# First mixer's recurrence: half a value product put between levels 0 and 1, two modulation chunks summed behind level 8, queries ahead of weight splits

## The reference, cut to what matters

```python
ada = jnp.einsum('bd,lde->lbe', jax.nn.silu(c), w_ada) + b_ada[:, None, :]   # 6 x 1024 modulation values
...
q = split_heads(jax.nn.silu(p[..., 3 * w:4 * w]), HG_HEADS) * (HG_DIM ** -0.5)
o_f, h_f = chunk_gla(q, k_f, v, logf_f, h0_f)          # S_t = diag(f_t) S_{t-1} + k_t v_t^T, o_t = S_t^T q_t
o_b, h_b = chunk_gla(flip_t(q), flip_t(k_b), flip_t(v), flip_t(logf_b), h0_b)
o = rmsnorm(o_f + flip_t(o_b), hg_gain.reshape(HG_HEADS, 1, HG_DIM))
o_hg = merge_heads(o) * jax.nn.silu(p[..., 4 * w:5 * w])
o_mlp = chunk_sgu(p[..., 5 * w:5 * w + MLP_WIDTH], p[..., 5 * w + MLP_WIDTH:], sgu_g, sgu_b, w_s, b_s)
...
x = x + g1 * (concatenate([o_hg, o_mlp]) @ w_out)
```

## Time and profile before

| what | value |
| --- | --- |
| median of 3 runs | 962.12 us (959.48 to 964.09) |
| the profiled execution | 960.85 us, span 959.0 us |
| TensorE busy | 927.3 us (97%) |
| VectorE busy | 740.5 us (77%) |
| ScalarE busy | 476.0 us (50%) |
| mean granted clock of TensorE | 0.995 |
| recurrence, level 0 to level 8 | 99.00 to 158.76 us of the span |

### The profile page before, as it was taken

The page is one execution under the profiler, slowest core; times in us unless marked ns, Lnnn a source line. Parts: engine busy times, 40 slices in busy tenths (PEclk is TensorE's granted clock), DMA queues, the critical chain, the costliest instruction groups (busy, mean ns, idle before and its releaser), DMA issues.

```text
span 959.0 us, 18956 instructions
## 1 busy us (share of the span) xinstructions
PE 927.3 (97%) x8174; PEld 872.4 (91%) x8174; DVE 740.5 (77%) x1101; ACT 476.0 (50%) x571; POOL 14.8 (2%) x34
## 2 busy tenths in 40 slices
PE   5999899999989999999999999999999999999997
PEld 3689899999989999989999899999999999999986
DVE  3689998889898988867957985535676987887863
ACT  3454445636545565458663753334645443334363
POOL 0000000002000000000200000000000000000000
PEclk8999999999999999999999999999999999999999
DMA  9988354465548656424654334333254565556541
GB/s 338 352 285 271 127 176 133 133 209 173 176 155 272 233 171 226 176 89 176 218 190 162 107 128 137 130 132 131 91 194 163 192 196 195 181 177 203 183 141 45
DMA packets 114051, 171.84 MB, mean 179 GB/s; under 512 B 3240, under 2 KB 96704, under 8 KB 109872
## 3 DMA queue, kind: packets, MB, share of 16 engines
q1 hardware_dynamic: 111680, 165.63, 51.4%
q0 software_dynamic: 1088, 2.57, 0.9%
q10 hardware_dynamic: 1200, 2.43, 0.7%
HBM read 169.55 MB, written 1.06 MB: 178 GB/s over the span
## 4 chain that ended last, share of the span: by engine, by line
PE 64%; DVE 8%; ACT 4%; issue 3%; DVEq 0%; ACTq 0%
PE bank L1171 20%; PE bank L1172 19%; PE bank L1173 19%; DVE wlo L629 3%; PE bank L1746 2%; ACT whi L620 2%; DVE arena L2307 1%; ACT arena L981 1%; DVE arena L2393 1%; DVE arena L1973 0%; DVE XT L2259 0%; PE bank L1280 0%; DVE raw L2049 0%; ACT arena L851 0%; PE bank L1210 0%
## 5 line engine op out<-in xcount | busy, mean ns | idle before, releaser
L1171 PE MATMUL bank<-hhi,whi 128*128 128x256 f32 (+1 forms) x1744 | 507.1, 291 | 7.5 <-issue 1.8
L1172 PE MATMUL bank<-hlo,whi 128*128 128x256 f32 (+1 forms) x1744 | 500.2, 287 | 0.0
L1173 PE MATMUL bank<-hhi,wlo 128*128 128x256 f32 (+1 forms) x1744 | 500.1, 287 | 0.0
L629 DVE TENSOR_TENSOR wlo<-raw,whi 128x2048 fp32r<-128x2048 f32 x131 | 299.7, 2289 | 109.7 <-ACT whi L620 84.1
L1171 PEld LDWEIGHTS bank<-hhi,whi 128*128 128x128 f32 x1744 | 334.0, 192 | 17.0 <-issue 11.9
L1172 PEld LDWEIGHTS bank<-hlo,whi 128*128 128x128 f32 x1744 | 334.2, 192 | 4.1 <-issue 1.2
L1173 PEld LDWEIGHTS bank<-hhi,wlo 128*128 128x128 f32 x1744 | 334.1, 192 | 2.5
L620 ACT ACTIVATE whi<-raw 128x2048 fp32r<-128x2048 f32 x131 | 250.1, 1913 | 139.7 <-PE bank L1173 127.3
L1171 PE MATMUL bank<-whi,hhi 128*128 128x256 f32 (+1 forms) x256 | 87.8, 343 | 0.8 <-ACT arena L1131 0.8
L1172 PE MATMUL bank<-wlo,hhi 128*128 128x256 f32 (+1 forms) x256 | 86.7, 339 | 0.0
L1173 PE MATMUL bank<-whi,hlo 128*128 128x256 f32 (+1 forms) x256 | 86.5, 338 | 0.0
(11 more groups left out here) (364 smaller groups left out, 805.9 us busy)
## 6 DMA issues: line engine op xcount, KB each, us to landing
raw<-in_w_up_dram SPq DMA_DIRECT2D x44, 1024.0 KB, 5.1
raw<-in_w_in_tiles_dram SPq DMA_DIRECT2D x32, 1024.0 KB, 4.9
raw<-in_w_down_dram SPq DMA_DIRECT2D x22, 1024.0 KB, 4.9
raw<-in_w_ada_dram SPq DMA_DIRECT2D x19, 1024.0 KB, 5.3
raw<-in_w_in_dram SPq DMA_DIRECT2D x14, 1024.0 KB, 5.3
raw<-in_w_branch_dram SPq DMA_DIRECT2D x6, 1024.0 KB, 5.1
arena<-in_w_ada_dram SPq DMA_DIRECT2D x10, 512.0 KB, 9.5
raw<-in_w_out_dram SPq DMA_DIRECT2D x4, 1024.0 KB, 5.1
```

What stands on the lines that cost most here:

```text
L629: dve.tensor_tensor(wlo[:, g % RING, :], raw[:, n % RING, :], whi[:, g % RING, :].bitcast(F32), ALU.subtract).then_inc(w_lo, 1)
L1171: pe.matmul(o, wh, ah, start=start, stop=False, **kw)
L1172: pe.matmul(o, wh, al, start=False, stop=False, **kw)
L1173: return pe.matmul(o, wl, ah, start=False, stop=stop, **kw)
```

## The change

Nothing is added or left out: the same instructions run in another order, on four engines.

1. TensorE: the first 24 of the 48 matmuls of v0a go between level 0 (with `ada_unit(2)`) and level 1, the other 24 stay behind level 1.
2. ScalarE: the split for q1's successor (mv0) and the copy of wsT go behind `mix_keys(1)`.
3. VectorE: the splits of mv0, mv1 and mu1 go from ahead of levels 2, 3 and 6 to behind these levels, that of gt0 from ahead of level 7 to behind level 8, that of gt1 from ahead of the normalisation of MV to behind it; level 7 goes ahead of `statistics(1)`; `weighted_late(15)` and `weighted_late(16)`, which stood behind levels 2 and 3, go behind level 8, the first right behind it, the second behind the normalisation of MV.
4. SyncE: the chunks 15 and 16 go three places back in the list each, which then reads mv1, mu0, mu1, 15, gt0, 16, gt1, 17.

```diff
@@ the list of chunks @@
-    for name in ("ff0", "ff1", "fb0", 8, "fb1", 9, 10, "q0", 11, "q1", 12, 13, 14, "v0", "v1", "mv0", 15, "mv1", 16,
-                 "mu0", "mu1", "gt0", "gt1", 17, "wo0", "wo1", "wo2", 18, "wo3", 19):
+    for name in ("ff0", "ff1", "fb0", 8, "fb1", 9, 10, "q0", 11, "q1", 12, 13, 14, "v0", "v1", "mv0", "mv1", "mu0",
+                 "mu1", 15, "gt0", 16, "gt1", 17, "wo0", "wo1", "wo2", 18, "wo3", 19):
@@ ScalarE @@
             for c in range(2):
                 unit_act(f"q{c}", Q[:, 2 * c:2 * c + 2, :], ACT.Silu)
-                split_hi(act, G[f"q{c}"] + RING)
                 if c == 0:
+                    split_hi(act, G["q0"] + RING)
                     tok_keys(0)
-            m_wait("wsT")
-            act.activation(wsT, m_bank("wsT")[:, :].rearrange("p (h q) -> p h q", h=HEADS), ACT.Copy
-                           ).then_inc(m_empty["act"], 1)
...
             mix_keys(1)
+            split_hi(act, G["q1"] + RING)
+            m_wait("wsT")
+            act.activation(wsT, m_bank("wsT")[:, :].rearrange("p (h q) -> p h q", h=HEADS), ACT.Copy
+                           ).then_inc(m_empty["act"], 1)
@@ TensorE @@
-            def gemm_tok(name, w, unit=None, t0=0):
+            def gemm_tok(name, w, unit=None, t0=0, part=(0, 1)):
 
                 wh, wl = w_parts(name, KT)
-                bk = g_open(unit or name)
-                for n in range(2):
+                bk = g_open(unit or name) if part[0] == 0 else g_bank(unit or name)
+                for n in part:
...
-                ins.then_inc(g_full, 1)
+                if part[-1] == 1:
+                    ins.then_inc(g_full, 1)
...
             level(0)
             ada_unit(2)
+            gemm_tok("v0", 512, "v0a", 0, part=(0,))
             level(1)
-            gemm_tok("v0", 512, "v0a", 0)
+            gemm_tok("v0", 512, "v0a", 0, part=(1,))
             level(2)
@@ VectorE @@
             level(1)
             modulation(2, g_wait("A2"), g_empty["dve"])
-            split_lo(dve, G["q1"] + RING)
             values(0, 0)
             level(2)
-            weighted_late(15)
+            split_lo(dve, G["q1"] + RING)
             values(0, 1)
+            level(3)
             split_lo(dve, G["v0"] + RING)
-            level(3)
-            weighted_late(16)
             values(1, 0)
...
             statistics(0)
+            level(6)
             split_lo(dve, G["mv0"] + RING)
-            level(6)
+            level(7)
             link(statistics(1))
...
             ins.then_inc(sg_stats, 1)
+            level(8)
+            weighted_late(15)
             split_lo(dve, G["mv1"] + RING)
-            level(7)
-            level(8)
-            split_lo(dve, G["mu0"] + RING)
             dve.wait_ge(sg_std, 1)
...
             dve.tensor_tensor(MV, MV, sgu_b.unsqueeze(1).broadcast_to([P, 2, 512]), ALU.add).then_inc(vn_ready, 1)
+            weighted_late(16)
+            split_lo(dve, G["mu0"] + RING)
             weighted_late(17)
             split_lo(dve, G["mu1"] + RING)
```

## The result

Changed kernel: median 976.38 us (972.75 to 978.71, 4 runs); before, 961.13 us (959.48 to 964.09, 4 runs). The ratio is 1.0142, with a 95% interval of 1.0117 to 1.0168: slower by 13.6 us (11 to 16). The forecast was 976, in a range of 970 to 980. In the changed kernel lines stand one to three further down than before (L1456 is oA's first matmul, L1422 a level's, L1407 level 8's, L1172 a product's first).

The account below looks back on a forecast made before the run. TensorE, busy 927.3 of 959.0 us, was taken as the bound, with VectorE also setting the pace behind level 8. wo0's split 14.7 us late, rounded to 14.5, gave 975.4 to 976.6; forecast 976, range 970 to 980.

Parts of the forecast that it names:

- the sum: From level 1 to wo0's split on VectorE: split starts at 188.8 against 174.06, 14.7 us late, rounded down to 14.5.
- Level 1: Ahead of level 1: 24 matmuls of v0a fill TensorE's wait; level 2 ends at 107.7 instead of 111.40, 3.7 us ahead.
- The bank of A2: Behind level 2: TensorE waits 3.0 us for modulation(2), plus 1.7 us for the lower clock; v0b ends 1.0 us behind.
- that case: Clock stays up ahead of v0b: the half product and lighter levels bring 1.8 us at level 8, instead of 0.1.
- the ten steps: Behind level 8: sum of 15, gt1's load and split, copies, square root, normalisation, sum of 16, wo0's load and split; 188.8.
- TensorE's slow restart at oA: At oA, started 10.1 us late: lower clock costs 1.7 us more, inside TensorE's wait for VectorE at wo0.
- steps 8 and 9: Ahead of wo0's split: sum of 16 (3.45 us), then wo0's load (5.3 us); without them the stretch is TensorE's, 10 to 12 late.
- The first: Rival behind level 8: ScalarE isn't held or gt1's load isn't late; wo0's split 7.2 us late, 969 us; chance 0.09.
- The second: Rival: A2's bank free by 107.7, TensorE's pace decides, sums lie in VectorE's idle time; 957 us; chance 0.02.
- The third: Rival behind wo0's split: slack in VectorE's stretch from 174.06 takes the 10 us back; 962 to 966 us; chance 0.03.
- Step 9: Behind the sum of 16: the load of wo0, 5.3 us from issue to landing, to 186.9.

Follow-up runs that it names:

- e1: The change, but chunks 15 and 16 and their weighted sums back where they stood before; 963.77 us, ratio 1.0007.
- e2: The change, but ScalarE splits gt1 behind the copies and the square root, not ahead of them; 968.98 us, ratio 1.0071.
- e9: The change, but the sum of 15 right ahead of VectorE's level 8, not behind it; 972.54 us, ratio 1.0100.
- e3: The change, but chunk 16 and its sum behind gt1 and gt1's split, both sums still behind level 8; 966.36 us, ratio 1.0043.
- e5: The kernel before with the half product alone (24 matmuls of v0a between level 0 and level 1); 962.55 us, ratio 1.0005.
- e7: The change with modulation(2) ahead of level 1, sum of 15 behind level 4, sum of 16 ahead of level 6, list reordered to match; 958.75 us, ratio 0.9959.
- e4: The change, but modulation(2), which empties A2's bank, ahead of VectorE's level 1; 969.53 us, ratio 1.0061.
- e6: The kernel before with only the list, the sums of 15 and 16 and the splits of gt0 and gt1 as in the change; 974.28 us, ratio 1.0131.
- e10: The kernel before with the half product and modulation(2) ahead of level 1; 963.03 us, ratio 1.0015.
- e8: As e7, but chunk 16 behind mu1 in the list and its sum ahead of level 7; 957.48 us, ratio 0.9959.

## Why the prediction was right

The mechanism held, and the size but for terms of 1 to 2 us; each step can be checked, from level 0's start (99.00 before, 99.31 after). That the median came within 0.4 us of 976 is luck: the four runs lie between 972.75 and 978.71. For the profiled execution the sum gave 975.4, and it took 978.71.

*Level 1.* The half product fills the wait, level 1 follows it without one. Level 2 was forecast for 106.9 and came at 107.85. A2 ended 0.4 us later than before (100.71), the two halves and level 1 took 0.4 us more than forecast, and TensorE waited 0.18 us for the queries, which VectorE ended 0.9 us later in this execution (L2135 at 107.60 against 106.69).

*The bank of A2.* Forecast: a wait of 3.0 us, and 1.7 us for the clock. Measured: 3.09 us, and v0b took from 111.69 to 119.89, 8.2 us against 5.8, so 2.4 us for the clock. This term was 0.7 us too small in this execution; in e1, e2 and e9 v0b took 7.3 us behind a wait of the same length, so 1.5 us. VectorE emptied the bank at 111.54, 0.9 us later than forecast, where level 0 was 0.3 us later. The two make up the error of the sum: level 8 was forecast for 156.7 and came at 158.31, 1.3 us later once level 0's 0.3 is taken off. I had charged the clock on top of the sum by the one row there was; e3 and e5 show that it can also stay up, and in e3 level 8 then came 1.7 us earlier than before (56.08 against 57.81), as the forecast had it for that case (1.8).

*Behind level 8.* From level 8's start to wo0's split the ten steps gave 188.8 - 156.7 = 32.1 us; it took 190.25 - 158.31 = 31.94 us. Singly: from the issue of gt1's load to ScalarE's split 5.13 us (5.3), oA a wait of 10.01 us, and 14.83 us behind level 8's start against 4.66 before, so 10.2 late (10.1), the sum of 16 with 3.44 us (3.45), wo0's load to ScalarE's split 5.27 us (5.3).

Two statements beside the ten steps were off. TensorE's slow restart at oA was put at 1.7 us: the first two of the four groups of output products took 3.54 and 2.69 us (173.14 to 176.68 to 179.37) and not 1.75, so 2.7 us; it lay inside VectorE's delay, as forecast. And without steps 8 and 9 the stretch was to be TensorE's, 10 to 12 us late. But in the change VectorE has its own work (the sum of 16, gt1's split, the sum of 17) up to 188.51 and waits only 1.74 us for wo0's split: with wo0 in time the stretch would have been VectorE's, and some 13 us late (an estimate: 188.51 - 158.31 - 17.25 = 12.95).

*The end.* From wo0's split on nothing was taken back, down to the first residual. The rest of the span is 761.4 us after and 759.7 before (976.9 - 215.47, 959.0 - 199.29). A stretch at the lower clock lies in it: from 434 to 446 us the granted clock is 0.86 in the change. The kernel e7, which is faster than before, has one at the same place of the program as well (0.79 from 416 to 424 us, where the kernel before has 1.00). The other kernels settle that the 1.7 us belong to the execution. Between 216 and 230 us behind the first residual the granted clock is 1.00 before and in e4, e5 and e6, and the rest of their spans takes 759.7 us; it is 0.88 in the change and in e1, e2, e3, e7, e9 and e10 (761.1 to 761.4 us), and 0.76 in e8 (762.5 us). e6 has the late loads and not the 1.7 us, e7 the 1.7 us and not the late loads. 15.9 + 1.7 + 0.3 us is the difference of the two spans, 17.9 us. Over all runs it is 13.6 us by the ratio.

*The rivals.* The first (ScalarE isn't held) falls by its wait of 11.05 us: the copies could have run at 160.26 and ran at 171.97, behind the split. Its time, 969, is that of e2 (968.98), where the mechanism was made. The second (the bank comes free in time and it gets faster) needed two edits: e4 alone doesn't make it faster, e7 does. What I priced at 957 came at 957.5 to 958.8. But I had let the two sums lie in VectorE's idle 3.32 and 3.54 us around level 8; e3, with the sums there, is 5.9 us late behind level 8, and e7 and e8 have them ahead of it. The third (slack behind) falls by the 25.22 us.

*What the experiments add.* I had left open how the 15.9 us divide. Of the 14.7 us behind level 8 (31.94 - 17.25), 7.5 are the copies, the square root and what follows them behind the waiting split (e2), 1.3 are VectorE's shorter wait for wo0's split (24.46 - 23.12, e3; 1.83 us in e2, 0.49 in e3), and 5.9 are left (23.12 - 17.25), of which 0.5 is still this wait and 5.4 VectorE's own work: it would have been late with every load in time. The division holds for this order of removal. Step 9 of the sum, 5.3 us long, is worth less than 2, as VectorE has other work to do in most of it. The other 1.2 us lie ahead of level 8. The prediction did not say that in the kernel before VectorE set the pace ahead of level 8 too: there the 3.7 us at level 2 go into waits for its queries even with the bank free (e10). In the change, whose sums have left these levels, they would have been gained (e4).

## What to carry to other kernels

Where weights go through a ring, a consumer that is moved back also moves back the load that takes its slot, and then whatever stands behind the wait for that load on an in-order engine: count from the moved instruction to the slot's next tenant, and from there along the queue in which this one is awaited. Side work belongs in the idle time of the engine that does it: one sum to a gap cost nothing here (e7, e8), both behind level 8 cost 5.9 us (e3). A product put into a wait is worth something only if its bank is free and the engine that is waited for isn't the one that sets the pace (e5, e10).

## What I had not expected of the hardware

*The clock at the start.* The lower clock at the start lasts for a different time in each execution, and when level 0 starts goes with it. The kernel before and e5_half_only, which differ only behind it, by stretches (length, busy us of each engine, granted clock, DMA):

```profile
15.00:25.00 10.00, 8.50 (x68) 4.95 (x68) 1.75 (x4) 0.98 (x3) 0.00 (x0) 0.66 1.10 365
25.00:35.00 10.00, 9.16 (x93) 6.08 (x93) 7.02 (x18) 2.13 (x5) 0.00 (x0) 1.00 1.09 377
```

```profile
15.00:25.00 10.00, 8.60 (x68) 4.94 (x67) 1.72 (x4) 0.89 (x3) 0.00 (x0) 0.59 1.10 364
25.00:35.00 10.00, 9.69 (x64) 6.36 (x64) 5.32 (x14) 1.02 (x3) 0.00 (x0) 0.56 1.09 378
```

From 25 to 35 us the one has the full clock (1.00), the other 0.56, and level 0 starts at 99.00 and at 102.13 us. All twelve traces fall into three groups by the time at which the matmuls of the start reach their shorter duration for good: about 16 us (e1, e4, e10; level 0 at 97.6 to 98.2), about 25 us (before, the change, e3, e6; 98.7 to 99.3) and about 34 us (e2, e5, e7, e8, e9; 102.0 to 102.6). These 4 to 5 us may well be a large part of the spread of 959 to 967 us that the runs of the kernel before show; it has one trace, so this isn't shown. A difference of 2 us needs many runs here, or a stretch of the trace.

The granted clock doesn't tell all of this. In the change it reads 1.00 throughout the first 99 us, yet 16 matmuls of L1225 take 1.89 us at 17.83 and at 23.05, and 1.04 us from 25.97 on, just as in the kernel before (L1224: 1.89 us at 17.73, where the granted clock is 0.76, and 1.05 at 25.76, where it is 1.00). So 1.00 at the start is no proof of the full clock, and durations of equal matmuls are the better witness. TensorE's 2.7 us more of busy time ahead of level 0 are of this kind.

*The clock behind a wait.* Whether it falls isn't told by the length of the wait alone. It fell behind 2.1 us (before, and e6_sums_only), 3.1 us (the change, e1, e2) and 3.0 us (e9), and stayed up behind 2.9 us (e3 and, ahead of level 4, e10) and 2.7 us (e5). Where it fell, v0b took 2.4 us longer in the change, 1.5 us in e1, e2 and e9, and v0a 1.4 us before.
